# The fourth tile of each weight unit's low part in the last feed-forward block, on GpSimd instead of VectorE

## The reference

```python
def swiglu(h, w_gate, w_up, w_down):
    return (jax.nn.silu(h @ w_gate) * (h @ w_up)) @ w_down

for i in range(DEPTH):                      # DEPTH = 4
    ...
    h = modulate(rms_norm(x, norm_gain[i, 1]), sh2, sc2)
    x = x + g2 * swiglu(h, ffn_w_gate[i], ffn_w_up[i], ffn_w_down[i])
```

## Time and profile before

| | |
|---|---|
| median of 3 runs | 2138.19 us (2136.71 to 2140.08) |
| the profiled execution | 2146.95 us, of which the span is 2145.2 us |
| TensorE matmul / VectorE / ScalarE / GpSimd busy | 1939.6 / 1343.0 / 918.0 / 112.0 us |
| low part of the weights, line 1439 | 237 instructions, 513.4 us |
| high part of the weights, line 939 | 230 instructions, 427.6 us |
| mean DMA rate over the span | 183 GB/s |
| the changed block within the span | about 1220 to 1436 us |

### The profile page before, as it was taken

One profiled execution on the slowest core, in us unless ns is written; L12 is line 12 of the kernel. 1 busy time (PEld: TensorE's weight loads), 2 busy tenths in 40 slices (PEclk: granted clock), 3 DMA queues, 4 the chain that ended last, 5 costly groups with the idle time before them and its releaser, 6 DMA issues.

```text
span 2145.2 us, 33126 instructions
## 1 busy us (share of the span) xinstructions
PE 1939.6 (90%) x13890; PEld 1510.3 (70%) x13890; DVE 1343.0 (63%) x1412; ACT 918.0 (43%) x1367; POOL 112.0 (5%) x139
## 2 busy tenths in 40 slices
PE   4888999999899998999899899989998888678999
PEld 3666887655777754777777677778777777666877
DVE  6776776573688734788645588865448545455565
ACT  3545443233544334544356544444336211335443
POOL 1001000110000010000000100001000220000000
PEclk9999999999999999999999999988999999989999
DMA  8763887553698731699743377963222000234553
GB/s 324 275 235 107 286 279 254 193 183 134 223 343 312 278 118 64 223 327 328 258 137 117 99 243 255 334 252 129 68 91 67 3 4 4 82 98 140 177 186 107
DMA packets 215401, 393.37 MB, mean 183 GB/s; under 512 B 11337, under 2 KB 130133, under 8 KB 199893
## 3 DMA queue, kind: packets, MB, share of 16 engines
q1 hardware_dynamic: 214741, 391.12, 52.6%
q0 software_dynamic: 512, 0.13, 0.0%
HBM read 390.17 MB, written 1.05 MB: 182 GB/s over the span
## 4 chain that ended last, share of the span: by engine, by line
PE 57%; DVE 23%; ACT 10%; issue 6%; DMA 2%; POOL 0%; DVEq 0%; ACTq 0%; SPq 0%; POOLq 0%
PE G L2146 12%; PE G L2148 11%; PE G L2147 11%; DVE w_lo L1439 11%; PE G L2352 5%; ACT w_hi L939 5%; DVE acc L1492 5%; PE G L2447 2%; PE A L2741 2%; DMA raw<-in_ffn_w_down 1%; ACT full L1004 1%; PE G L2755 1%; DVE act_st L1777 1%; PE A L2753 1%; DVE n_st L1549 1%
## 5 line engine op out<-in xcount | busy, mean ns | idle before, releaser
L1439 DVE TENSOR_TENSOR w_lo<-raw,w_hi 128x2048 fp32r<-128x2048 f32 (+2 forms) x237 | 513.4, 2166 | 306.5 <-ACT w_hi L939 296.3
L939 ACT CAST w_hi<-raw 128x2048 fp32r<-128x2048 f32 (+1 forms) x230 | 427.6, 1859 | 556.3 <-PE G L2148 495.3
L2146 PE MATMUL G<-w_hi,h_hi 128*128 128x512 f32 (+2 forms) x1232 | 494.5, 401 | 25.4 <-DVE w_lo L1439 10.6
L2147 PE MATMUL G<-w_lo,h_hi 128*128 128x512 f32 (+2 forms) x1232 | 483.4, 392 | 0.0
L2148 PE MATMUL G<-w_hi,h_lo 128*128 128x512 f32 (+2 forms) x1232 | 482.7, 392 | 0.0
L1492 DVE SCALAR_TENSOR_TENSOR acc<-raw,c_col,acc 128x2048 f32<-128x2048 f32 x120 | 282.0, 2350 | 45.2 <-DMA raw<-in_ada_w 24.3
L2146 PEld LDWEIGHTS G<-w_hi,h_hi 128*128 128x128 f32 x1232 | 236.9, 192 | 81.3 <-issue 35.8
L2146 PE MATMUL G<-w_hi,act_hi 128*128 128x512 f32 (+2 forms) x624 | 245.9, 394 | 29.6 <-DVE w_lo L1439 24.1
L2148 PEld LDWEIGHTS G<-w_hi,h_lo 128*128 128x128 f32 x1232 | 236.0, 192 | 50.2
L2147 PEld LDWEIGHTS G<-w_lo,h_hi 128*128 128x128 f32 x1232 | 237.1, 192 | 45.6
L2147 PE MATMUL G<-w_lo,act_hi 128*128 128x512 f32 (+2 forms) x624 | 242.5, 389 | 0.0
(11 more groups left out here) (402 smaller groups left out, 2098.0 us busy)
## 6 DMA issues: line engine op xcount, KB each, us to landing
raw<-in_ada_w SPq DMA_DIRECT2D x96, 1024.0 KB, 5.2
raw<-in_ffn_w_gate SPq DMA_DIRECT2D x88, 512.0 KB, 3.9
raw<-in_ffn_w_up SPq DMA_DIRECT2D x88, 512.0 KB, 5.0
raw<-in_ffn_w_down SPq DMA_DIRECT2D x40, 1024.0 KB, 5.8
raw<-in_w_mlp SPq DMA_DIRECT2D x32, 1024.0 KB, 5.4
raw<-in_w_ada SPq DMA_DIRECT2D x24, 1024.0 KB, 5.5
raw<-in_w_in SPq DMA_DIRECT2D x18, 1024.0 KB, 5.4
raw<-in_sb_w_in SPq DMA_DIRECT2D x32, 512.0 KB, 4.9
```

The costliest lines, as they stand in the source:

```text
L939: nc.scalar.copy(w_hi[:, c % 2, 0:len(kts), 0:n], raw[:, slot].rearrange("p (k n) -> p k n", k=UNIT_K)[:, 0:len(kts), 0:n])\
L1439: return nc.vector.tensor_tensor(w_lo[:, c % 2, ks, 0:n], raw[:, slot].rearrange("p (k n) -> p k n", k=UNIT_K)[:, ks, 0:n], w_hi[:, c % 2, ...
L2146: nc.tensor.matmul(banks[t][:, 0:n], x_hi[:, kt, ts], w_hi[:, u % 2, i, 0:n], start=st, stop=False)
L2147: nc.tensor.matmul(banks[t][:, 0:n], x_hi[:, kt, ts], w_lo[:, u % 2, i, 0:n], start=False, stop=False)
```

## The change

`shared` lists the full units among the last 30 units ahead of `u_lat`: all of the block from its third panel on, 28 units. For these, VectorE's `low_part` covers row tiles 0 to 2 (1536 columns) and GpSimd computes tile 3 (512 columns) with an instruction of the same form. GpSimd waits for the same two semaphores as VectorE does and raises `lo_pool`. VectorE waits for `lo_pool` before it frees the slot of `raw`, and TensorE waits for it before the unit. Nothing else is moved; the arithmetic is the same.

```diff
+        lo_pool = sem("lo_pool")
...
+        load_of = dict(zip(range(len(units)), [i for i, load in enumerate(loads) if load[0] != "ada"]))
+        shared = [u for u in range(u_lat - 30, u_lat) if len(units[u][2]) == UNIT_K]
+        nth_shared = {u: i for i, u in enumerate(shared)}
...
+            for u in shared:
+                c, slot, ks = nth_converted[u], load_of[u] % RING, UNIT_K - 1
+                pool.wait_ge(hi_ready, c + 1)
+                pool.wait_ge(gemm_done, converted[c - 2] + 1)
+                nc.gpsimd.tensor_tensor(w_lo[:, c % 2, ks, 0:512], raw[:, slot].rearrange("p (k n) -> p k n", k=UNIT_K)[:, ks, 0:512],
+                                        w_hi[:, c % 2, ks, 0:512].bitcast(F32), ALU.subtract).then_inc(lo_pool, 1)
...
-                low_part(c, slot, slice(0, len(kts)), n).then_inc(lo_ready, 1)
+                low_part(c, slot, slice(0, len(kts) - (u in nth_shared)), n).then_inc(lo_ready, 1)
                 dve.wait_ge(lo_ready, c + 1)
+                if u in nth_shared:
+                    dve.wait_ge(lo_pool, nth_shared[u] + 1)
                 dve.sem_inc(raw_free, 1)
...
+                if k.u in nth_shared:
+                    pe.wait_ge(lo_pool, nth_shared[k.u] + 1)
                 k.u += 1
                 pe.wait_ge(hi_ready, u + 1)
                 pe.wait_ge(lo_ready, u + 1)
```

## The result

The changed kernel takes 2146.78 us (median of 8 runs, 2142.46 to 2151.47) against 2138.15 us for the kernel before (2135.99 to 2140.09): a ratio of 1.0040, 95% interval 1.0027 to 1.0053. The profiled execution took 2147.54 us, its span is 2145.7. That profile alone would mislead: the profiled execution of before took 2146.95 us, almost as long, because it lay far above its own median. The whole spans can't be subtracted here; the changed block has to be cut out.

The account below looks back on a forecast made before the run. The path was taken as ScalarE, five VectorE steps and two TensorE units; serial delays at TensorE's waits, 0.26 + 1.14 + 0.6 + 0.26 + 0.3 + 0.38 - 0.27 = 2.7 us, gave 2140.9 us, range 2135.0 to 2148.0.

Parts of the forecast that it names:

- The bound: Changed block: the path is ScalarE, five VectorE steps, two TensorE units; VectorE's two low parts are on it.
- the places of the earlier trace: Eight waits of TensorE, 16.7 us in all, for the low part and `act_mul`; only delays reaching these move the end.
- Series, not side by side: VectorE and GpSimd reading two SBUF tensors each run in series; rival side by side: -6.9 us, 2130.5 us, chance 0.10.
- The price of GpSimd's part: GpSimd's 128x512 tensor_tensor takes 1.04 us, 0.91 in series; VectorE's low part drops 0.53 to 1.76.
- The handover: GpSimd's end reaches VectorE in 0.10 us, where VectorE's own end took 0.22.
- +0.26, 0 and +0.31: VectorE's delay when the high part comes while it idles, during the step just ahead, or during `acc` with `acc_c` ahead.
- the first four places: TensorE's waits before 1252.08, 1272.77, 1297.34 and 1317.52: +0.26, +0.57, +0.57 and +0.6 us.
- +0.38 drowns in that: Between 1318 and 1362 TensorE's units find the low part 1.0 us ready or more, so +0.38 us costs nothing.
- The clock: Rival: same serialisation, but grown waits bring two more half-clock stretches of 1.5 us: 5.7 us, 2143.9 us, chance 0.33.
- where a wait passes about 1.8 us: The clock rival's condition: TensorE waits of 1.43 and 1.44 would grow to some 2.0 us, 1.84 to 2.1.
- The down part: At 1362 to 1424, loads issued later mostly wait less in the DMA queues: between 0 and 0.6 us, taken as 0.3.
- The forecast and the range: Whole kernel: +2.7 us on the median, 2140.9 us; range 2135.0 to 2148.0; serial sum's chance 0.42.

Follow-up runs that it names:

- the cleared tiles: The changed kernel with every wait kept, but GpSimd fills its tile of the low part with zeros instead of subtracting: 2129.84 us, ratio 0.9945 to before.
- the runs of the two parts: Kernel before with the change for the 18 gate and up units alone, 2145.47 us (1.003), or the 10 full down units alone, 2139.12 us (0.9997).

## Why the prediction was right in kind and too small

**The bound.** Right in the main. The loss appears at the places of the earlier trace rows, though also at three that the prediction had ruled out (below), and a shorter low part alone is worth 0.2 to 0.7%. The shortcut that it suggests, a quarter less on VectorE is a quarter less on the path, is what fails.

**Series, not side by side.** Right, at full size for `acc` and `acc_c` too, which the earlier trace rows had shown only small. Serial order, 0.04 us between the two starts, and an overlap of fixed parts are in the timeline as the earlier trace rows had them. The rule of the Trainium skill, "SBUF — State Buffer", "Who interferes with whom", on VectorE instructions with two SBUF inputs agrees with the 3.38 us of `acc_c`; its exception for a GpSimd instruction that only writes agrees with the 0.53 us of the cleared tiles, beside which nothing was stretched.

**The price of GpSimd's part.** This is the main term that was mis-sized: "A GpSimd tensor_tensor of 128x512 takes 1.04 us". It takes 1.26. The row was of another operand pattern, and I did not ask which. The page "GPSIMD Engine Reference" of the Trainium skill, section "3.1 Elementwise — side-by-side cycle accounting", gives 4497 ns for 2048 columns; a quarter of that, as an estimate, is 1.12 us, which would have spoken against 1.04. In the runs here half of the columns cost more than half of the time (256 took 0.74 us where 512 took 1.26), so such a quarter is still too low.

**The handover.** Sized 0.10 us from the earlier trace rows, it measured 0.20 (1260.18 to 1260.38). With 0.22 more for the price and 0.10 for the handover, the prediction's +0.26, 0 and +0.31 for VectorE become +0.58, +0.20 and +0.53; measured are +0.60 (3.11 - 2.51), +0.22 (2.76 - 2.54) and +0.50 (3.38 - 2.35 less 0.53). Its own sum over the first four places, made with the measured ones, is (0.60 + 0.22) + 1.10 + 1.10 + (0.5 + 0.50) = 4.0 us, against 4.87 measured and 2.0 predicted.

**"Between 1318 and 1362 TensorE has no wait ... +0.38 drowns in that."** Wrong. The units had 1 us to spare; the transposes had not. I looked at the units' wait for the low part and not at the four transposes between them, which wait for `act_mul`. In before `act_mul` ended 0.06 us ahead of them:

```profile
1329.64 0.76 DVE L1777 TENSOR_TENSOR act_st<-G,silu_st 128x256 f32<-128x256 f32 x2 [0.22 <-DVE w_lo L1439]
1330.46 0.66 PE L2482 MATMUL A<-consts,act_st 128*128 128x128 f32 x4
```

So +0.60 on `act_mul` is +0.53 on TensorE, three times with 0.53, 0.53 and 0.67: 1.7 us. Together with the 4.0 that is 5.7 us for the gate part, and the change in that part alone measured 6.2 us (2145.47 - 2139.31, with an interval from 3.9 to 9.2).

**The clock.** The rival's mechanism is in the profile of after: a stretch of 3.4 us at half clock behind the wait that grew from 1.44 to 1.96 us, and a longer one behind the fourth. From 1317.52 to 1364.28 the shift grew by 3.5 us, 1.7 of them the new waits and about 1.7 the 3.4 us more at half clock. But the down part had 3.4 us less of it, and it differs from execution to execution. The length of the wait alone doesn't tell whether half clock follows: in after it followed waits of 1.96 and 2.30 us and not those of 2.09 and 3.04, and in before it did not follow that of 2.49. So the prediction's "where a wait passes about 1.8 us" doesn't hold.

What all runs together say of the clock I had overlooked. The mean granted clock was 0.9625 on average over the eight runs after (0.959 to 0.965), and 0.9646 over 29 runs of the kernel before (0.961 to 0.967), those beside the runs of the two parts. As an estimate from these, 0.0021 / 0.5 of 2146 us is 9 us more at half clock in each execution, which would cost up to half of that, 4.5 us. The runs of before directly beside the change have no clock on record, except the profiled 0.962, so this is an indication and not shown. It leaves the rival open as a part of the 8.6 us: the sum, corrected, gives the gate part's loss without it, but not the whole.

**The down part.** Not contradicted: for the late loads between 0 and 0.6 us was said, for all places from 1364.28 on 0.7; -0.2 was measured, with an interval from -3 to +2. That is too wide to tell these apart.

**The forecast and the range.** 2140.9 us said, 2146.8 found: +8.6 us where the sum had +2.7. The chances were 0.49 for a change too small to tell, 0.39 for slower and 0.12 for faster, so what came was not what the prediction held likeliest. The range, up to 2148.0, held it with room made by the rival of the clock (2143.9) and not by its sum; with the price and the transposes wrong, that was partly luck.

## What to carry to other kernels

Before an idle GpSimd is given part of a VectorE instruction, count the SBUF inputs of both: if they run one behind the other, the shared piece costs GpSimd's price on the path, which is higher than VectorE's for the same columns (here 1.26 us against 0.53), and it also stretches whatever VectorE does next. A price is taken from a row with the same operand pattern, and every consumer of a delayed step is asked for its slack, not only the one that was seen waiting. And look at the small gaps first: taking out the separate semaphore increments behind VectorE's long instructions, in all layers, gained 17 us here, where a shorter low part in this block could gain some 7.

## What the runs showed of the hardware that I had not expected

- GpSimd's tensor_tensor of 128x512 takes 1.26 us with two full inputs, whether it multiplies or subtracts and whether it writes float32 or fp32r, and 1.04 us when the second input repeats one element.
- On VectorE a separate increment behind a long instruction and its wait cost about 0.2 us, the wait by itself nothing that can be seen: gaps of 0.22 to 0.25 us went to 0.03. Without those behind the low parts and the modulation steps the kernel was 0.85% faster.
- A GpSimd instruction that only writes (0.53 us for 128x512) didn't disturb VectorE in any of 28 places.
